# The last norms before a layer's input projection, moved into the projection's first chunk of weights

## The reference, cut to what matters

```python
# the end of an FFN: its output y is normed, gated and added to the stream x
x = x + gate * rms_norm(y, g_out)
# the start of the next mixer: x is normed, scaled and shifted, and multiplied by the input weights
h = modulate(rms_norm(x, g_in), shift, scale)        # h * (1 + scale) + shift
proj = h @ w_in                                      # 1024 x 2752
```

## Time and profile before

| | us |
|---|---|
| median of 3 runs | 4042.0 |
| lowest and highest | 4037.34, 4047.2 |
| the profiled execution | 4041.85 |
| its span (first to last instruction) | 4040.0 |
| PE busy in it | 3524.7 (87%) |
| DVE busy | 1763.5 (44%) |
| ACT busy | 1610.6 (40%) |
| POOL busy | 563.0 (14%) |

### The profile page before, as it was taken

One profiled execution on the slowest core, in us unless ns is written; L12 is line 12 of the kernel. 1 busy time (PEld: TensorE's weight loads), 2 busy tenths in 40 slices (PEclk: granted clock), 3 DMA queues, 4 the chain that ended last, 5 costly groups with the idle time before them and its releaser, 6 DMA issues.

```text
span 4040.0 us, 56176 instructions
## 1 busy us (share of the span) xinstructions
PE 3524.7 (87%) x20726; PEld 2916.4 (72%) x20726; DVE 1763.5 (44%) x2518; ACT 1610.6 (40%) x2756; POOL 563.0 (14%) x943
## 2 busy tenths in 40 slices
PE   4998776898599999999997999766996789999997
PEld 3998553676377888888887999444775568888886
DVE  3111664776544532542454111664775445324322
ACT  3111544776443532432453110554776344223222
POOL 0000454221212100100100000443211111000000
PEclk8999876999699999999998999877998799999999
DMA  4223522000614323322444132522003223234223
GB/s 180 71 86 135 184 58 58 6 8 18 245 58 141 104 89 113 125 99 91 157 164 149 63 94 92 219 61 58 8 5 119 82 99 115 86 100 142 94 91 106
DMA packets 145417, 401.14 MB, mean 99 GB/s; under 512 B 15696, under 2 KB 79888, under 8 KB 138384
## 3 DMA queue, kind: packets, MB, share of 16 engines
q1 hardware_dynamic: 112848, 328.45, 24.3%
q0 software_dynamic: 11712, 43.00, 2.9%
q10 hardware_dynamic: 20736, 28.18, 2.0%
HBM read 337.32 MB, written 57.02 MB: 98 GB/s over the span
## 4 chain that ended last, share of the span: by engine, by line
PE 71%; DVE 7%; ACT 5%; issue 5%; DMA 5%; PEld 3%; DVEq 1%; POOLq 1%; POOL 1%; SPq 1%; ACTq 0%; PEldq 0%
PE psum L789 17%; PE psum L790 17%; PE psum L791 17%; PE psum L1043 6%; PE psum L1071 4%; PE psum L1058 2%; DVE part L1770 2%; DVE region L2103 1%; PE psum L996 1%; DMA region<-in_ffn_out 1%; PE psum L979 1%; DMA proj<-region 1%; DMA region<-proj 1%; PEld psum L789 1%; PEld psum L791 1%
## 5 line engine op out<-in xcount | busy, mean ns | idle before, releaser
L789 PE MATMUL psum<-part,part 128*128 128x512 f32 (+2 forms) x4240 | 1518.3, 358 | 104.0 <-DVE part L1770 97.8
L790 PE MATMUL psum<-part,part 128*128 128x512 f32 (+2 forms) x4240 | 1506.8, 355 | 0.0
L791 PE MATMUL psum<-part,part 128*128 128x512 f32 (+2 forms) x4240 | 1506.2, 355 | 0.0
L1770 DVE TENSOR_TENSOR part<-region,part 128x1024 fp32r<-128x1024 f32 (+5 forms) x446 | 561.3, 1260 | 1040.3 <-ACT part L1597 534.3
L789 PEld LDWEIGHTS psum<-part,part 128*128 128x128 f32 x4240 | 806.4, 190 | 210.4 <-issue 109.7
L790 PEld LDWEIGHTS psum<-part,part 128*128 128x128 f32 x4240 | 806.6, 190 | 96.3 <-issue 3.4
L791 PEld LDWEIGHTS psum<-part,part 128*128 128x128 f32 x4240 | 805.8, 190 | 94.0
L1597 ACT CAST part<-region 128x1024 fp32r<-128x1024 f32 x220 | 230.7, 1049 | 461.5 <-PE psum L791 436.7
L2103 DVE TENSOR_REDUCE region<-psum 128x1 f32<-128x1280 f32 (+1 forms) x216 | 295.3, 1369 | 168.8 <-PE psum L1043 168.8
L1503 ACT ACTIVATE region<-psum,region 128x1280 f32<-128x1280 f32 (+1 forms) x216 | 266.7, 1235 | 92.4 <-DVE region L2103 92.1
L1840 DVE COPY region<-psum 128x344 f32<-128x344 f32 x80 | 41.2, 516 | 521.2 <-PE psum L791 374.7
(11 more groups left out here) (222 smaller groups left out, 3299.4 us busy)
## 6 DMA issues: line engine op xcount, KB each, us to landing
region<-in_ffn_in SPq DMA_DIRECT2D x220, 512.0 KB, 3.3
region<-in_ffn_out SPq DMA_DIRECT2D x80, 704.0 KB, 4.1
region<-in_ada_w SPq DMA_DIRECT2D x14, 2048.0 KB, 9.9
proj<-region ACTq DMA_DIRECT2D x16, 1720.0 KB, 11.4
region<-proj SPq DMA_DIRECT2D x20, 1376.0 KB, 9.2
region<-in_w_in SPq DMA_DIRECT2D x16, 1376.0 KB, 7.3
region<-in_ada_w SPq DMA_DIRECT2D x20, 1024.0 KB, 7.0
region<-proj SPq DMA_DIRECT2D x116, 128.0 KB, 2.2
```

The costliest lines, as they stand in the source:

```text
L789: mm(out, a[0], b[0], start=start, stop=False)
L790: mm(out, a[0], b[1], start=False, stop=False)
L791: return mm(out, a[1], b[0], start=False, stop=stop)
L1770: return v.tensor_tensor(lo, x, hi.bitcast(F32), ALU.subtract)
```

## The change

- `norm(0)` and `norm(2)` are no stages any more, and their two handovers go. `norm(4)`, at the very end, stays as it was.
- The loads of the first two chunks of weights move to the start of `project`. For the first layer SP waits for `x_summed` first, since the weights' slots lie over the squares.
- The first pair of chunks, u = 0, is written out ahead of the loop on PE, ACT and DVE; the loop runs over u = 1..3 (on PE) and u = 1, 2.
- First layer: the tokens are taken in three pieces, 0 to 511, 512 to 1023 and 1024 to 1279. The first piece is normed before anything else of the projection. The second is normed by DVE and ACT at j = 0 of chunk 0, the third at j = 1. PE waits for `h_ready` ahead of tiles 0, 4 and 8.
- Second layer: the weights of chunk 0 are split first. `grow` comes at j = 0 on DVE, the squares at j = 0 and 1 on ACT, `sum_x` on PE behind tile 4, the root at j = 2 on ACT, `norm_h` at j = 2 on DVE, `round_h` at j = 3 on ACT. PE waits for `h_ready` ahead of tile 8.
- In chunk 0 the weights of chunk 1 are split at j = 3, not 2.
- `X_AT` moves up past the chunk's output. In the first layer x then lies over the small operands, so SP issues `small(0)` only when all 24 steps of `scale_h` are through (`h_normed`). `wgate` is set to zero by DVE at j = 2 of chunk 0, and `small`'s last two loads wait for that.

```diff
-        X_AT = R_A + 2 * KD * N
+        X_AT = Y1 + (4 * KD + NT) * IN_C
...
+                self.pieces = [span] if has_y else [(a, a + n) for a, n in spans(0)]
+                self.h_before = KD * sum(len(r.pieces) for r in RENEWALS if r.pre is not None)
...
             def project(l):
+                if l == 0:
+
+                    sp.wait_ge(sem("x_summed"), 1)
+                for s in range(2):
+                    load_win(l, 0, s)
+                if l == 0:
+
+                    sp.wait_ge(sem("h_normed"), len(RENEWALS[0].pieces) * KD)
                 small(l)
...
+                r = alone(2 * l)
                 if r.has_y:
                     sum_y(r)
...
+                for s in range(2):
+                    pe.wait_ge(sem("win_ready"), l * IN_CHUNKS + s + 1)
+                    for tt in range(NT):
+                        if s == 0:
+                            for i, (a, _) in enumerate(r.pieces):
+                                if a == tt * P:
+                                    pe.wait_ge(sem("h_ready"), ready(r) + i + 1)
+                        tile(0, s, tt)
+                        if s == 0 and tt == 4 and r.has_y:
+                            sum_x(r)
+                with pe.Fori(1, IN_CHUNKS // 2) as u:
...
-                        if j == 2 and not is_last:
+                        if between:
+                            between(j)
+                        if j == (3 if between else 2) and not is_last:
                             part(u + s, 1 - s)
                         act.wait_ge(sem("in_made0"), l * 40 + u * 10 + n + 1)
...
+                r = alone(2 * l)
+
+                def between(j):
+
+                    if not r.has_y:
+                        if j + 1 < len(r.pieces):
+                            for k in range(KD):
+                                round_h(r, k, j + 1)
+                    elif j < 2:
+                        if j == 0:
+                            root(r.y_root(), "y_summed", r.grown, "y_root")
+                        for k in range(4 * j, 4 * j + 4):
+                            square(r, k)
+                    elif j == 2:
+                        root(r.x_root(), "x_summed", r.given, "x_root")
+                    elif j == 3:
+                        for k in range(KD):
+                            round_h(r, k)
+                if not r.has_y:
+                    for k in range(KD):
+                        round_h(r, k)
                 part(0, 0)
-                with act.Fori(0, IN_CHUNKS // 2 - 1) as u:
+                chunk(0, 0, False, between)
+                chunk(0, 1, False)
+                with act.Fori(1, IN_CHUNKS // 2 - 1) as u:
...
+            def norm_h(r, p=0):
+                for k in range(KD):
+                    scale_h(r, k, p)
+                    if k >= 1:
+                        rest_of_h(r, k - 1, p)
+                rest_of_h(r, KD - 1, p)
+                dve.drain().then_inc(sem("h_ready"), 1)
...
+                def between(j):
+
+                    if not r.has_y:
+                        if j + 1 < len(r.pieces):
+                            norm_h(r, j + 1)
+                    elif j == 0:
+                        for k in range(KD):
+                            grow(r, [k])
+                    elif j == 2:
+                        norm_h(r)
+                    if j == 2:
+                        v.memset(wgate, 0.0).then_inc(sem("wgate_zero"), 1)
+                if not r.has_y:
+                    norm_h(r)
                 part(0, 0)
```

More of the change, by code:

```diff
@@ L251, in alone, with ready @@
             return renewals(i // 2 - 1, True)[-1] if i else RENEWALS[0]
+        def ready(r):
+            return sum(len(alone(2 * i).pieces) for i in range(DEPTH) if alone(2 * i).index < r.index)
         class Weave:
@@ L779, in _ @@
                     project_back(l, block_)
-                norm(2 * l + 2)
+            norm(2 * DEPTH)
         @block.tensor
@@ L1829, in part, with chunk @@
                          ).then_inc(sem("win_ready"), 1)
-                def chunk(u, s, is_last):
+                def chunk(u, s, is_last, between=None):
                     for j in range(5):
                         n = 5 * s + j
-                        if j == 2 and not is_last:
+                        if between:
+                            between(j)
+                        if j == (3 if between else 2) and not is_last:
                             part(2 * u + s + 1, 1 - s)
@@ L1841, in chunk @@
                                       ).then_inc(sem("in_kept1"), 1)
+                r = alone(2 * l)
+                def between(j):
[3 more added lines that the diff above has]
+                    elif j == 0:
+                        for k in range(KD):
+                            grow(r, [k])
+                    elif j == 2:
[4 more added lines that the diff above has]
+                    norm_h(r)
                 part(0, 0)
-                with dve.Fori(0, IN_CHUNKS // 2 - 1) as u:
+                chunk(0, 0, False, between)
+                chunk(0, 1, False)
+                with dve.Fori(1, IN_CHUNKS // 2 - 1) as u:
                     for s in range(2):
@@ L2468, in store_x, with grow @@
                 pool.dma_start(dst, r.x(k)).then_inc(sem("x_out"), 16)
-            def norm(i):
+            def grow(i):
                 r = alone(i)
[L2472 to L2476, removed]
+                load_x(r)
+                for k in range(KD):
+                    store_x(r, k)
+                pool.wait_ge(sem("x_out"), 16 * KD * (r.grown + 1))
                 handover("pool", pool)
@@ L2501, in _ @@
             idle()
-            norm(0)
             pool.wait_ge(sem("const_in"), 16 * 7)
             for l in range(DEPTH):
-                idle()
+                if l:
+                    grow(2 * l)
+                else:
+                    idle()
                 prepare(l)
@@ L2515, in _ @@
                 idle()
-                norm(2 * l + 2)
+            grow(2 * DEPTH)
 def constants():
```

73 lines of the change are left out of this document (28 added, 45 removed).

## The result

The changed kernel takes 4007.6 us (median of 4 runs, 4004.3 to 4011.4), the kernel before 4043.0 beside it. The ratio is 0.9914, 95% interval 0.9896 to 0.9931: 35 us less, by the interval 28 to 42. A second series gave 0.992 (0.9897 to 0.9943). The forecast of 4011 lies 3.4 us above the median.

What follows compares the result with a forecast made beforehand. PE, busy 87%, was taken as the bound, its chunk 0 starts waiting for norm and weights' split in series. 13.3 + 21.1 - 3.4 = 31.0 us off 4041.85 gave 4010.9, forecast 4011, range 4005 to 4021.

Steps and rivals of the forecast that it cites:

- The place of the gain: Both projections: PE's start of chunk 0 sets the end, which gains what the start gains, less work added to PE's path.
- The sum's net terms: First layer's start 13.3 us earlier; second layer's 21.1 us earlier, less 3.4 us for the sum of squares; 31.0 in all.
- The first piece: First layer: norm of 512 tokens, then weights' split; PE starts at 69.5 instead of 82.8, 13.3 us gained.
- The weights between the layers: Second layer: weights land at 2189.2, PE starts 5.7 us later, at 2194.9 instead of 2216.0, 21.1 us gained.
- The sum of squares on the path: Second layer: `sum_x` between tiles 4 and 5 costs PE 3.4 us, bounds 3.4 and 6.9.
- The ninth tile: Second layer, tile 8 waiting for `h_ready`: cover 0.8 to 2.1 us, costed at nothing, 0 to 3 for the range.
- The price of the miss: Tile 8's wait: up to 3 us costs itself; beyond, the clock falls and a half-speed start costs another 2.4 us.
- Rival 1: Second layer: tile 8 waits for `h_ready`, price 2 to 7 us, 4013 to 4018; chance 0.2.
- The table load's drain: ACT's root ahead of tile 8: by the skill's 2.66 us a switch, tile 8 waits 2 us, 4013 instead of 4011.
- Rivals 2 and 3: The former: weights or norm late, 4 to 10 us lost, 4015 to 4021, chance 0.08; the latter: see rival 3.
- rival 3: Chunk 0: copy waits keep PE's clock at half, 29 us more a chunk; chance 0.04 for one, 0.03 for both.
- the rise at 5.2 us behind both starts: Both projection starts at half clock: 18 matmuls at 0.287 us and 6 at 0.157, tile 0 in 6.1 us.

Runs made afterwards that it cites:

- only_first: Changed kernel with only the first layer's norm woven in, the norm between the layers a stage with its barrier again: ratio 0.9966 against the kernel before.
- only_second: Changed kernel with only the norm between the layers woven in, the first norm a stage with its barrier again: ratio 0.9963 against the kernel before.
- unrolled_only: Changed kernel with both norms stages again; written-out code, x's new place and the small operands' wait remain: ratio 0.9999 against the kernel before.
- four_pieces: Changed kernel with the first layer's tokens in pieces of 256, 256, 512 and 256: ratio 0.9897 against the kernel before.
- dve_adds: Changed kernel with VectorE adding up x's eight squares and TensorE summing one tensor, 2 records instead of 16: ratio 0.9913 against the kernel before.
- the two kernels that use it up: Changed kernel with x's sum of squares moved behind the sixth tile (4017.65 us, one run) or behind the eighth (4015.41 us, one run).
- all_three: Changed kernel with the edits of four_pieces, dve_adds and early_split together: 3997.0 us, ratio 0.989 against the kernel before.
- sum_behind_8: Changed kernel with x's sum of squares moved behind the second layer's eighth tile, right ahead of the ninth: 4015.41 us, one run.
- early_split: Changed kernel with the first layer's chunk 0 weights loaded and split already in the first modulation: ratio 0.9909 against the kernel before.

## Why the prediction was right

**The place of the gain.** It said that each stretch is as long as the wait for its first tile, and that all behind moves with that tile. `only_first` and `only_second` show each part on its own, and `unrolled_only` shows that nothing else in the change moves the time. The mean lengths of the stretches over all profiles that treat them alike are 342.7 and 329.1 in the first layer (four and six profiles), 343.4 and 326.0 in the second (four and five): 13.5 and 17.4 us. The sum's net terms were 13.3 and 17.7, 31.0 in all against 30.9; that the total fits so closely is partly luck, since the two differences, 0.2 and 0.3 us, have opposite signs.

**The first piece.** Forecast 18.2 us from the first scale to the first tile (69.5 less 51.26), measured 17.9. The scaled steady part (1.58 a step) is what the steps at 58.43, 60.00 and 61.58 in the trace show. The prediction speaks of seven such steps, 11.1 us, but its sum takes six, the 9.5 in it, and the sum is what the trace bears out: ACT's cast starts 12.3 us behind the first scale, forecast 12.5. `four_pieces` confirms the term: with the first piece halved, DVE is through with it in 7.0 us instead of 13.3.

**The weights between the layers.** Landing, cast and start came as the row had them: ACT's cast 5.8 us behind the barrier, the tile 5.7 behind the cast.

**The sum of squares on the path.** Forecast 3.4, measured 3.3; `dve_adds` takes 2.7 of it away.

**The ninth tile.** The cover was given as 0.8 to 2.1 us, by whether ACT's table load runs behind or ahead of the wait for the sum. It ran ahead, at 2194.70, ten us before that wait ended at 2205.21, and the cover is 2.0 by the two kernels that use it up. The price of the miss was right as well in the two places tried: 1.7 us of wait cost 1.5, and 9.3 us, in which the clock fell, cost 2.5 more than themselves, forecast 2.4. That 3 us is the border between the two is not shown; no run had a wait between 1.7 and 9.3 us there, and the last section has a fall of the clock without any rest. Rival 1 did not come true here, and is real one tile further on.

**The table load's drain.** By the Trainium skill, "ScalarE: Activation LUTs", section "What ACT_TABLE_LOAD costs", each switch should have taken 2.66 us. In the trace of after exp starts 1.30 us after its load begins (2205.71 to 2207.01), and the norm's first scale 2.2 us after the wait's end. The measurement decides: 1.3 us a switch, and none of it where the load can run ahead of a wait.

**What was not in the sum.** The 37.5 us between the two profiled spans are 31 and the scatter of single executions, with the first modulation's 2.9 in it, which goes the other way. The medians, 35 us apart with 28 to 42 for the interval, are compatible with the sum alone; whether a little of the 4 us over it is real these runs don't tell. The range was laid around the forecast with the scatter of medians in it, and that held.

**Rivals 2 and 3.** No load came late: the ten small loads were issued right behind the second chunk's and delayed nothing that was due. In chunk 0 PE never waited for a copy; in the profile of after it did so once in each layer, in a later chunk, for 0.4 and for 0.8 us. The condition of rival 3, rests before the clock has risen, never came about, so what the clock would do then stays untested. The sum took the rise at 5.2 us behind both starts. It came 4.3 us behind the first (76.4) and 5.8 behind the second (2185.8), by the granted clock of these two stretches:

```profile
76.00:78.00 2.00, 2.00 (x13) 2.00 (x12) 2.00 (x4) 1.22 (x2) 0.00 (x0) 0.91 0.00 0
...
2185.00:2186.00 1.00, 1.00 (x5) 1.00 (x5) 0.93 (x3) 0.00 (x0) 0.54 (x1) 0.60 0.37 131
```

## What to carry to other kernels

Where a preparation and a first product stand in series behind a barrier, look at how much of the preparation the first tile needs: the start follows the length of the first piece (13.3 us for 512 tokens, 6.9 for 256), and the rest can lie beside the tiles as long as each piece's length is under the time of the tiles that run meanwhile. Price a wait that breaks a running TensorE off in two parts: the wait itself and, if the clock falls in it, a start at half clock on top, here 2.5 us. How long a rest may be before that happens is not settled here: 1.7 us of it left the clock up, and 9.3 us did not, where it fell 3.4 us into the rest. Judge the difference of two profiled spans stage by stage, against a second profile of the same kernel, before any of it is explained.

## What the runs showed that was not expected

The clock also fell while TensorE was busy. The last product of the first modulation is 32 matmuls of two columns, back to back. It takes 3.73 us at the full clock in `all_three` and as long in the profile of before, and 5.73 us in that of after; the granted clock shows why (after, then before):

```profile
48.00:50.00 2.00, 2.00 (x16) 2.00 (x16) 0.00 (x0) 0.00 (x0) 0.00 (x0) 0.77 0.00 0
50.00:52.00 2.00, 2.00 (x11) 2.00 (x11) 0.00 (x0) 0.00 (x0) 0.00 (x0) 0.50 0.00 0
```

```profile
48.00:50.00 2.00, 2.00 (x20) 2.00 (x20) 0.00 (x0) 0.00 (x0) 0.00 (x0) 1.00 0.00 0
```

Where the product is short, the clock can fall right behind it, with no rest before: in the profile of before the product ends at 50.5, and so does the full clock.

```profile
50.00:50.50 0.50, 0.50 (x5) 0.41 (x4) 0.00 (x0) 0.00 (x0) 0.00 (x0) 0.98 0.00 0
50.50:51.00 0.50, 0.00 (x0) 0.00 (x0) 0.38 (x3) 0.00 (x0) 0.00 (x0) 0.50 0.00 0
```

So the fall 3.0 us after the sum, from which the prediction priced a wait, is not what follows on every kind of work.

Of 13 profiles four (after, `sum_behind_8`, `unrolled_only`, `early_split`) have the long form of the product, of kernels whose code is the same there but for addresses or, in `early_split`, for work on other engines. The four have also the shortest `prepare` of the first layer, 99.8 to 100.2 us against 100.9 to 102.7 in the nine others. The two go together in these profiles, and what one stage loses the other gives back; whether both hang on how the clock happened to stand to the work is a guess, and why the product comes in two forms these runs don't show.
